# Layer norms by token tile in a two-layer hybrid decoder kernel: scale and offset moved from GpSimd to VectorE, and the router computed by token

## The reference

```
for l in range(2):
    h = hybrid_mixer(x, ...)                       # projections, three mixers, merge, @ w_out
    x = layer_norm(DN_ALPHA * x + h, ln1_g[l], ln1_b[l])
    f = swiglu(x, ...) if l == 0 else moe_swiglu(x, router_w, ...)   # 8 experts, top 2
    x = layer_norm(DN_ALPHA * x + f, ln2_g[l], ln2_b[l])

layer_norm(x, g, b) = (x - mean) * rsqrt(var + 1e-5) * g + b      # over the 1024 channels
moe_swiglu: logits = x @ router_w ; the two best experts of a token, softmax over the two
```

## Time and profile before

| what | value |
|---|---|
| median of 3 runs | 1886.59 us (1884.95 to 1887.59) |
| the profiled execution's own time | 1885.17 us |
| its span (first to last instruction) | 1883.4 us |
| busy: PE, DVE, ACT, POOL | 92%, 73%, 53%, 2% of the span |
| mean granted TensorE clock | 0.969 of full |
| chain that ended last, by engine | PE 78%, DVE 14%, ACT 4%, issue 4%, DMA 1% |
| moved by DMA | 411.29 MB, mean 218 GB/s |

### The profile page before, as it was taken

The page is one execution under the profiler, slowest core; times in us unless marked ns, Lnnn a source line. Parts: engine busy times, 40 slices in busy tenths (PEclk is TensorE's granted clock), DMA queues, the critical chain, the costliest instruction groups (busy, mean ns, idle before and its releaser), DMA issues.

```text
span 1883.4 us, 27888 instructions
## 1 busy us (share of the span) xinstructions
PE 1731.8 (92%) x10784; PEld 1532.1 (81%) x10784; DVE 1368.5 (73%) x1242; ACT 1002.6 (53%) x919; POOL 31.1 (2%) x20
## 2 busy tenths in 40 slices
PE   6898998879999789899989599999999999999996
PEld 6797897868999679888888488888888888888885
DVE  5757755675444676766475688989898988888887
ACT  4363243633333344523344376767676776767674
POOL 0000000001000200000000100000000000000000
PEclk9899999998999799999999799999999999999998
DMA  8322322464665343223234598989999999999993
GB/s 262 114 91 90 112 86 91 136 179 134 178 178 178 122 147 112 90 88 93 68 121 168 190 351 321 374 318 379 330 374 331 356 337 360 331 362 354 342 364 121
DMA packets 252061, 411.29 MB, mean 218 GB/s; under 512 B 8400, under 2 KB 133840, under 8 KB 251344
## 3 DMA queue, kind: packets, MB, share of 16 engines
q1 hardware_dynamic: 249440, 400.68, 61.6%
q10 hardware_dynamic: 2544, 9.54, 1.4%
HBM read 408.09 MB, written 2.10 MB: 218 GB/s over the span
## 4 chain that ended last, share of the span: by engine, by line
PE 78%; DVE 14%; ACT 4%; issue 4%; DMA 1%; SPq 0%; DVEq 0%; ACTq 0%
PE W L428 16%; PE W L430 16%; PE W L429 16%; PE Y L428 5%; PE Y L429 5%; PE Y L430 5%; PE Y L596 2%; PE Y L590 2%; PE Y L785 2%; ACT w_hi L952 2%; DVE w_lo L1330 2%; PE W L505 1%; DVE sc L1475 1%; PE Y L505 1%; DVE xt L1492 1%
## 5 line engine op out<-in xcount | busy, mean ns | idle before, releaser
L428 PE MATMUL W<-w_lo,x_hi 128*128 128x512 f32 (+1 forms) x1120 | 393.0, 351 | 9.1 <-DVE x_lo L1629 6.5
L430 PE MATMUL W<-w_hi,x_hi 128*128 128x512 f32 (+1 forms) x1120 | 387.6, 346 | 0.0
L429 PE MATMUL W<-w_hi,x_lo 128*128 128x512 f32 (+1 forms) x1120 | 386.9, 345 | 0.0
L1330 DVE TENSOR_TENSOR w_lo<-raw,w_hi 128x2048 fp32r<-128x2048 f32 x115 | 263.2, 2292 | 165.7 <-ACT w_hi L952 164.6
L1337 DVE TENSOR_TENSOR w_lo<-raw,w_hi 128x2048 fp32r<-128x2048 f32 x144 | 329.7, 2290 | 52.5 <-ACT w_hi L958 52.3
L958 ACT ACTIVATE w_hi<-raw 128x2048 fp32r<-128x2048 f32 x144 | 276.0, 1917 | 83.3 <-PE Y L430 43.7
L428 PE MATMUL W<-x_lo,w_hi 128*128 128x256 f32 x992 | 294.2, 297 | 22.1 <-DVE w_lo L1330 15.7
L1337 DVE TENSOR_TENSOR w_lo<-raw_more,w_hi 128x2048 fp32r<-128x2048 f32 x120 | 275.0, 2291 | 32.0 <-ACT w_hi L958 31.9
L429 PE MATMUL W<-x_hi,w_lo 128*128 128x256 f32 x992 | 285.7, 288 | 0.0
L430 PE MATMUL W<-x_hi,w_hi 128*128 128x256 f32 x992 | 285.4, 288 | 0.0
L958 ACT ACTIVATE w_hi<-raw_more 128x2048 fp32r<-128x2048 f32 x120 | 230.7, 1922 | 67.1 <-PE W L430 43.9
(11 more groups left out here) (278 smaller groups left out, 2097.7 us busy)
## 6 DMA issues: line engine op xcount, KB each, us to landing
raw<-w_in SPq DMA_DIRECT2D x124, 512.0 KB, 4.7
raw<-moe_gate SPq DMA_DIRECT2D x48, 1024.0 KB, 7.0
raw<-moe_up SPq DMA_DIRECT2D x48, 1024.0 KB, 7.7
raw<-moe_down SPq DMA_DIRECT2D x48, 1024.0 KB, 6.2
raw_more<-moe_gate SPq DMA_DIRECT2D x40, 1024.0 KB, 7.5
raw_more<-moe_up SPq DMA_DIRECT2D x40, 1024.0 KB, 7.3
raw_more<-moe_down SPq DMA_DIRECT2D x40, 1024.0 KB, 6.9
raw<-w_branch SPq DMA_DIRECT2D x24, 512.0 KB, 4.4
```

The lines of the kernel that those rows point to most:

```text
L428: nc.tensor.matmul(out_ap, lhs[0], rhs[1], start=start, stop=False)
L429: nc.tensor.matmul(out_ap, lhs[1], rhs[0], start=False, stop=False)
L430: return nc.tensor.matmul(out_ap, lhs[0], rhs[0], start=False, stop=stop)
L1330: V.tensor_tensor(w_lo[u % 3][:], raw[u % 3][:], w_hi[u % 3][:].bitcast(F32), ALU.subtract)\
```

## The change

The norms are done one token tile at a time.

- TensorE, `out_part` and `out_units`: of the four units of `w_out`, the first is used for both tiles; then units 1 to 3 for tile 0 alone (`sum_done`), then units 1 and 2 for tile 1, then the transposes of tile 0, then unit 3 for tile 1. The transposes of a tile go to the `Y` banks that held its sums.
- VectorE, `layer_norm(m, t, ...)`: per tile the moments, then `(x - mean) * g`, the reciprocal, and `* rstd + b` on `xtok`, as the last norm already did. `turned_lo` makes `x_lo` from the PSUM banks, two instructions a tile; ScalarE's `ln_turned` makes `x_hi` from them. `feature_major`, `ln_split` and GpSimd's `scale_xtok` are gone, and with them every wait for `xtok_ready`.
- `first_pair` takes both of its units for tile 0, then transposes tile 1, then both for tile 1.
- Before norm 2 the first two expert tiles are no longer split; on VectorE their splits now stand after it. The places of the expert tiles exchange `raw0` and `raw1`, so that the first tile lands in `raw1`.
- The router takes `xf` as the stationary operand, 8 matmuls of 8 columns a tile, those of tile 0 before the transposes of tile 1; the copy to `facc` and the two small transposes are gone.
- Norm 3: tile 0 is finished before the moments of tile 1 begin.

```diff
-PLACES = ((0, 0), (0, 1), (1, 0), (1, 1))
+PLACES = ((1, 0), (1, 1), (0, 0), (0, 1))
...
+            def out_units(l, u):
+
+                out_part(l, 0, u, 0)
+                out_part(l, 0, u, 1).then_inc(w_used, 1)
+                for q in range(1, 4):
+                    last = out_part(l, q, u + q, 0)
+                last.then_inc(sem("sum_done"), 1)
+                for q in range(1, 3):
+                    out_part(l, q, u + q, 1).then_inc(w_used, 1)
+                norm_transposes(2 * l, 0)
+                out_part(l, 3, u + 3, 1).then_inc(w_used, 1)
...
+            def norm_transposes(m, t):
+
+                pe.wait_ge(sem("xn_ready"), NT * m + t + 1)
+                for k in range(KD):
+                    last = transpose(tiles(Y[2 * t + k // 4][:], 4)[:, k % 4, :], xtok[:, t, k * P:(k + 1) * P])
+                    if k % 4 == 3:
+                        last.then_inc(sem("xnt_done"), 1)
...
+            def first_pair(u, i, g, fresh):
+
+                gate_up(u, i, (0, 2 * g), (0,), fresh)
+                gate_up(u + 1, i, (1, 2 * g + 1), (0,))
+                norm_transposes(0, 1)
+                gate_up(u, i, (0, 2 * g), (1,), fresh)
+                gate_up(u + 1, i, (1, 2 * g + 1), (1,))
...
             pe.wait_ge(sem("cmo_full"), 32)
-            for k in range(KD):
-                if k % 2 == 0:
-                    pe.wait_ge(sem("xf_ready"), 9 + k // 2)
-                last = nc.tensor.matmul(Y[0][0:NE, 0:T], rt_s[:, k, :], xf[:, k, :], start=k == 0, stop=k == KD - 1)
-            last.then_inc(sem("router_done"), 1)
-            pe.wait_ge(sem("router_ready"), 1)
             for t in range(NT):
-                last = nc.tensor.transpose(Y[1][:, t * NE:(t + 1) * NE], facc[0:NE, 0, t * P:(t + 1) * P], ident[0:NE, 0:NE])
+                if t:
+                    norm_transposes(2, t)
+                pe.wait_ge(sem("xf_ready"), 2 * t + 2)
+                for k in range(KD):
+                    last = nc.tensor.matmul(W[0][:, t * NE:(t + 1) * NE], xf[:, k, t * P:(t + 1) * P], rt_s[:, k, :],
+                                            start=k == 0, stop=k == KD - 1)
...
-            pe.wait_ge(sem("xtok_ready"), 3)
             experts(MOE_U0, 0)
...
+            def ln_turned(m, t):
+
+                dst, name = (xf, "xf_ready") if m == 2 else (x_hi, "x_hi_ready")
+                for h in range(2):
+                    act.wait_ge(sem("xnt_done"), 4 * m + 2 * t + h + 1)
+                    A(dst[:, 4 * h:4 * h + 4, t * P:(t + 1) * P], tiles(Y[2 * t + h][:], 4), ACT.Copy).then_inc(sem(name), 1)
...
+                ln_scale(2 * l, 0)
+                if l:
+                    ln_turned(2, 0)
+                    split_expert(MOE_U0, 0, 0, 0)
+                    ln_scale(2, 1)
+                    split_expert(MOE_U0, 1, 0, 0)
+                    ln_turned(2, 1)
+                    continue
+                split_hi(MIX_UNITS)
+                ln_turned(0, 0)
+                split_hi(MIX_UNITS + 1)
+                split_hi(MIX_UNITS + 2)
+                ln_scale(0, 1)
+                ln_turned(0, 1)
...
-            def scale_xtok(m, t):
-
-                pool.wait_ge(sem("gb_full"), 16 * (m + 1))
-                pool.wait_ge(sem("xnt_done"), 4 * (m + 1))
-                link(nc.gpsimd.tensor_tensor(xtok[:, t, :], xtok[:, t, :], gb[:, 0, :], ALU.mult))
-                last = nc.gpsimd.tensor_tensor(xtok[:, t, :], xtok[:, t, :], gb[:, 1, :], ALU.add)
...
+            def normalise(m, t, src):
+
+                x_t = xtok[:, t, :]
+                dve.wait_ge(sem("gb_full"), 16 * (m + 1))
+                link(V.scalar_tensor_tensor(x_t, src[:, t, :], small[:, 80 + 2 * t:81 + 2 * t], gb[:, 0, :],
+                                            ALU.subtract, ALU.mult))
+                dve.wait_ge(sem("ln_sd_ready"), NT * m + t + 1)
+                link(V.reciprocal(small[:, 54 + t:55 + t], small[:, 50 + t:51 + t]))
+                return V.scalar_tensor_tensor(x_t, x_t, small[:, 54 + t:55 + t], gb[:, 1, :], ALU.mult, ALU.add)
...
+            def turned_lo(m, t):
+
+                for h in range(2):
+                    dve.wait_ge(sem("x_hi_ready"), 4 * (m + 1) + 2 * t + h + 1)
+                    part = slice(4 * h, 4 * h + 4), slice(t * P, (t + 1) * P)
+                    V.tensor_tensor(x_lo[:, part[0], part[1]], tiles(Y[2 * t + h][:], 4),
+                                    x_hi[:, part[0], part[1]].bitcast(F32), ALU.subtract).then_inc(sem("x_lo_ready"), 1)
...
+                layer_norm(2 * l, 0, 0)
+                if l:
+                    layer_norm(2, 1, MOE_U0)
+                    split_expert(MOE_U0, 0, 0)
+                    split_expert(MOE_U0, 1, 0)
+                    continue
+                split_lo(MIX_UNITS)
+                turned_lo(0, 0)
+                split_lo(MIX_UNITS + 1)
+                layer_norm(0, 1, MIX_UNITS)
+                turned_lo(0, 1)
...
+                layer_norm(1, 0, 0)
+                layer_norm(1, 1, layer_unit(1))
+                turned_lo(1, 0)
+                turned_lo(1, 1)
```

More of the change, by code:

```diff
@@ L494, in units @@
                 if kind == "out":
[L495 to L496 removed]
+                    out_units(l, u0)
                 elif kind.startswith("branch"):
@@ L705, in att_out, with gate_up @@
                         last.then_inc(sem("att_done"), 1)
-            def norm_transposes(m):
-                for t in range(NT):
-                    pe.wait_ge(sem("xn_ready"), NT * m + t + 1)
-                    for k in range(KD):
[L712 to L718, removed]
+            def norm_transposes(m, t):
[4 more added lines that the diff above has]
+                        last.then_inc(sem("xnt_done"), 1)
+            def gate_up(u, i, f, ts=range(NT), fresh=None):
                 unit_ready(u, i)
@@ L975, in units @@
                 if kind == "out" or kind.startswith("branch"):
[L976 to L980 removed]
+                    for q in range(a, 2 if kind == "out" else b):
+                        split_hi(u0 + q + 2)
                     return
@@ L1286, in _ @@
                 experts(END_U, NE, True)
-            ln_scale(3)
+            for t in range(NT):
+                ln_scale(3, t)
         @block.gpsimd
@@ L1617, in layer_norm @@
[L1617 to L1642 removed]
+                mark(V.bn_aggr(small[:, 80 + 2 * t:82 + 2 * t], small[:, 56 + 12 * t:68 + 12 * t]),
+                     "ln_var_ready", NT * m + t + 1)
@@ new lines, in layer_norm @@
+            def layer_norm(m, t, used):
+                if t == 0:
+                    dve.wait_ge(sem("sum_done"), m + 1)
+                else:
+                    dve.wait_ge(w_used, used)
+                moments(m, t, xtok, (Y[2 * t][:], Y[2 * t + 1][:]))
+                mark(normalise(m, t, xtok), "xn_ready", NT * m + t + 1)
+            def turned_lo(m, t):
+                for h in range(2):
+                    dve.wait_ge(sem("x_hi_ready"), 4 * (m + 1) + 2 * t + h + 1)
+                    part = slice(4 * h, 4 * h + 4), slice(t * P, (t + 1) * P)
+                    V.tensor_tensor(x_lo[:, part[0], part[1]], tiles(Y[2 * t + h][:], 4),
+                                    x_hi[:, part[0], part[1]].bitcast(F32), ALU.subtract).then_inc(sem("x_lo_ready"), 1)
@@ L1848, in _ @@
             link(V.engine_nop())
-            dve.wait_ge(sem("gb_full"), 64)
-            layer_norm(3, facc)
+            for t in range(NT):
+                moments(3, t, facc)
+                normalise(3, t, facc).then_inc(sem("out_ready"), 1)
 def constants():
```

209 lines of the change are left out of this document (61 added, 148 removed).

## The result

| | before | changed |
|---|---|---|
| median of 4 runs each, same chip | 1887.09 us (1884.95 to 1889.59) | 1872.89 us (1871.41 to 1875.15) |
| profiled execution, its span | 1885.17, 1883.4 us | 1872.82, 1871.0 us |
| busy PE, DVE, ACT, POOL | 92, 73, 53, 2% | 93, 72, 54, 0% |
| mean granted clock | 0.969 | 0.965 |

The ratio is 0.9909, with a 95% interval of 0.9881 to 0.9937. The change is faster, but by 14 us where the forecast had 28, and 1872.9 lies outside its range of 1854.5 to 1866.

The account below looks back on a forecast made before the run. TensorE was taken as the bound, with standstills and half clock at the norms. Savings of 12.7 (norm 0), 6.3 (norm 1) and 8.8 (norm 2) summed to 27.8 us, forecasting 1858.8 us; range 1854.5 to 1866.

Parts of the forecast that it names:

- The rests on `w_lo`, tile 0 and tile 1: First norm: TensorE waits 1.5 us for the third w_out unit's low part, 0.5 for tile 0, 2.4 for tile 1.
- the routing instructions: Router's chain on VectorE: without GpSimd the two slow instructions take 0.16 us each, saving 3.7.
- Rivals 2 and 4: Expert stage: weight stream takes back 8.8 us (1868, chance 0.08); exchanged buffers make tiles land late (1890, chance 0.03).
- Rival 3: Low parts come late behind weight splits; TensorE stands 2 to 3 us more at norms 0 and 2; 1864, chance 0.08.
- Norm 0: From the w_out projections through the first feed-forward pair: overlapping the token tiles saves 12.7 us.
- In this sum the clock holds through the gap: Gap of 420.2 to 424.6 before the second tile's feed-forward: full clock assumed; a fall would cost 1.5 to 2.5 us.
- rival 1: Clock stays at half longer: first norm's gap (1.5 to 2.5 us), counting and gather (3.0); about 1864, chance 0.17.
- The row that was set against it: Third norm, before: clock rose just after the router's first matmul, 3 us after transposes began; taken to suggest transposes count.
- Norm 2: Second layer's w_out projections through router, counting and gather: saves 8.8 us, or 5.8 if the clock is not back.
- I take the clock to be back by the counting matmuls: After the router: at full clock counting saves 1.0 us and the gather 2.0; otherwise nothing.
- Elsewhere: Rest of the kernel: GpSimd's passes hid nothing else, experts get the same work, swapping raw0 and raw1 only renames buffers.
- Norm 1: Norm before the lora unit: saves 6.3 us, 5.7 to 6.9, with the clock back after 4.5 us.

Follow-up runs that it names:

- fill_norms: Changed kernel with dummy matmuls in TensorE's rests of norms 0 and 2: 1863.77 us, ratio 0.986.
- experiments 3 and 5: Small dummy matmuls in chain and finish: changed kernel 1866.86 us, before 1888.1; dummies behind layer 1's lora unit: changed kernel 1868.7 to 1876.3, kernel without overlap 1879.4.
- fill_all: Changed kernel with dummy matmuls in TensorE's rests of norms 0, 1 and 2 and in chain and finish: 1857.4 us, ratio 0.9829.

## Why the prediction was wrong

- **The mechanism and the order of steps were right.** The rests on `w_lo`, tile 0 and tile 1 lie where they were put, within 0.4 us, and their lengths agree within 0.2; `x_lo` from PSUM took the 0.69 assumed; the routing instructions lost 3.7. Rivals 2 and 4 (experts' transfers) are out: no change in that stage. Rival 3 (halves do not overlap) is out by norm 0's 47.2.
- **Norm 0: right in its steps; that the clock holds was a matter of luck.** "In this sum the clock holds through the gap": it held in two profiles of three of the change (47.2, 12.7 saved; four of seven with the variants) and fell in the one of the result, which cost 2.7. That is rival 1; it had 0.17 where three of seven profiles fell, and its price of 1.5 to 2.5 was a little low. The Trainium skill's statement in "TensorE: Matmul & The Clock Gate", Part 4, that transposes are no work for the gate, fits the fall at 427 right behind eight transposes. It would not tell why the clock held in four profiles with the same eight transposes and the same rests. The row that was set against it leaned less than was said: at norm 2 before, the first eight transposes began at 1047.65, 6 us ahead of the clock's rise, not 3.
- **Norm 2: "I take the clock to be back by the counting matmuls" failed.** It was at half until 1058.5, so counting and gather gained nothing: 3.0 (rival 1 again). The other two profiles of the change had it at half through counting too, and for 3.0 of the gather's 5.25. A fall in `w_out` at 1021 to 1024, behind the 2.36 us rest that the change itself made there, cost 1.6 more: from this unit's start to the transposes of tile 0 it took 13.47 us (1019.59 to 1033.06), and 11.85 in `fill_norms`.
- **"Elsewhere" was put at nothing, and that failed; it is the largest single part.** The unchanged mixers took 7.5 us more in this pair. 2.8 of it was chance. The 4.7 of mixer 1 (5.4 in the means) came with the change, which does not touch this code: it moved the mixer's thin steps to where the clock fell for them (experiments 3 and 5, with what they leave open). Nothing in one profile of before could size it, but the profile shows that these steps are thin, and a term "0 to 6 for stages that are moved" belonged in the range.
- **The base was off too.** The profiled execution of before took 1885.17, where 61 runs have a median of 1890.1. With the fair base the saving is 18.0, not 14.2, against the 27.8 of the sum; a forecast from it would have been 1862, 10 us off instead of 14.
- **Norm 1: near**, 5.2 in the means and 5.9 in this pair, for 6.3.

The sum itself describes what the change is worth when TensorE's clock is kept up in the norms: in `fill_norms` the three norms took 12.7, 5.6 and 9.9 us less than in the first profile of before, 28.2 for 27.8. The 32 us of `fill_all` are more than the change's own, since its dummies also raise the clock in steps that the sum left as they were; before with dummies in its norms was not run, so how much of that before could have had as well is not known.

## What to carry to other kernels

Before an overlap of steps is written, look for an engine that slows another: moving GpSimd's passes onto VectorE without any overlap (`serial`) gave as much as the whole change. When a change makes or moves rests of TensorE, count the clock as a term of its own, with both levels, for every stage behind it that TensorE fills thinly, the unchanged ones too; and keep TensorE on dummy matmuls through rests of known length, which was worth 15 us here (1872 to 1857). Compare stages between landmarks of several executions: one profile of each kernel could not have told that 2.8 of the 7.5 us were chance and the rest was not.

## What the runs showed of the hardware

- The same code with the same rests ran at full clock in some executions and at half in others: the part up to the first `w_out` matmul, the same in the versions without dummies in it, took 387.8 to 396.5 us, with 17 to 41 us at half clock; whole runs of one kernel spread over 1861.3 to 1876.6.
- With 2.3 us of dummy matmuls ahead of it and nothing else altered, a stage took 360.7 us instead of 354.5 (one profile each), and the kernel 8.3 us more.
- A gather of 16 float32 matmul pairs by token took 3.84 us at full clock, 5.72 with 4.0 of them at half, and 6.57 with 5.8 at half; eight 128x128 transposes took 1.09 at full and 1.97 at half.
